# Eighteen of a layer's 96 gathered dot products split into a product on GpSimd and a sum on ScalarE, and the gate stage begun four blocks sooner

## The chip, the core and the metric

The program runs on one core of a Trainium2 chip. The metric is the device time of one execution in microseconds. In the profile the engines are PE (TensorE matmuls), PEld (its weight loads), DVE (VectorE), ACT (ScalarE), POOL (GpSimd) and SP (SyncE, which here only issues DMAs).

## What is computed

A trunk of two layers over 256 tokens of width 1024. Each layer has a mixer (attention and pooling in layer 0, a gated MLP in layer 1) and then a product-key channel mixer with 16384 experts, which takes most of the time and is the only part the change touches:

```python
q = (ht @ w_q).reshape(T, PEER_HEADS, 2, PEER_HALF_DIM)
scores = jnp.einsum('thic,hikc->thik', q, sub_keys)
sv, si = lax.top_k(scores, PEER_TOPK)
cand = sv[:, :, 0, :, None] + sv[:, :, 1, None, :]
best, ci = lax.top_k(cand.reshape(T, PEER_HEADS, 256), PEER_TOPK)
expert = (i1 * 128 + i2).reshape(T, 128)          # 8 heads x 16 picks
gate = jax.nn.softmax(best, axis=-1).reshape(T, 128)
hid = jax.nn.gelu(jnp.einsum('cd,ckd->ck', xb, w_down[eb]))
out = jnp.einsum('ck,ckd->cd', gb * hid, w_up[eb])
```

## The kernel before, in words

**Dense and gathered tokens.** Of the 256 tokens, 160 are handled densely: TensorE multiplies them with all 16384 experts, in 128 "down" blocks of 128 experts (`down(b)`, eight matmuls of 160 columns, which the trace counts as 16), and later 128 "up" blocks. The other 96 tokens are handled through gathered rows: 64 of them (two half-sets of picks on 128 partitions, 64 rows of the ring, "sparse") and 32 "later" tokens (four partitions sets, 32 rows, "more"). For each of these 96 rows GpSimd issues an indirect DMA that brings 128 expert rows of 1024 floats (512 KB) into a slot of a ring of ten (`gather(q)`), and VectorE takes one dot product per partition with `scalar_tensor_tensor` and an accumulator (`dots`, L1548). The other factor is `h_rows` in PSUM for sparse rows and `more_rows` in SBUF for more rows. In the up stage 96 more rows are gathered and added up with their coefficients (L1665).

**How a down block is handed on.** Three PSUM banks serve the down blocks in turn. `down(b)` waits until block b-3 has been taken out of its bank. In ScalarE's loop over b, the step for b first takes block b-2 through Gelu (`take_hidden(b - 2)`, L849, up to block `G_FROM - 1`; `activate_hidden`, L854, from there on), and then does what is hung on that b: the exponentials at b = 18 and 54 (`EXP_AT`), the row numbers, ten `write_ones` from b = 16 (`ONES_FROM` = 12 plus 4), the take-over of the later tokens' row numbers at b = 33, and so on. ScalarE also issues the odd loads of the down weights from n = 40 on.

**Retrieval on VectorE.** While TensorE goes through the down blocks, VectorE finds the picks, first of token tile 0 and then of tile 1. Tile 0's picks give the row numbers. During tile 1 there are 14 places at which some dots are put between the retrieval's instructions (`early_dot`): four in the first top-16 search, two in the second, eight in the loop that looks up the pick numbers (`L1601`). Place i does the dots up to `early_after(i)`. In total `EARLY` = 40 are done there, 18 sparse rows and then 22 of the later tokens' rows.

**The gate stage.** When both tiles are found (`idg_done`), TensorE turns numbers and gates round ahead of block `IDS_AT` = 77, VectorE splits them into two indices (`ids_split`), and from block `G_FROM` = 80 on, each down block is followed by the gates of four tokens (`token_gates(g)`, four matmuls of one-hot operands), 40 groups in all, to block 119. A group's operands are made by GpSimd (`build_first`, L629), ScalarE (`finish_one_hots`) and VectorE. The remaining 56 dots are spread over the blocks from `G_FROM` + 1 on, 56 in 44 blocks (`dots_after`).

**GpSimd's order.** In each layer it first asks for `EARLY + RING - 1` = 49 rows, then builds the operands of group 0, 1, ..., with later gathers between. `gather(q)` for q of 10 or more waits until row q-10, which had the slot, has been used, and until row q-5 has landed:

```python
for q in range(asked):
    gather(q)
pool.wait_ge(ids_split, l + 1)
for g in range(TGROUPS):
    build_first(g)
```

Lines printed by the profile: L613 gather, L629 first one-hots on GpSimd, L849 and L854 hidden values on ScalarE, L982 all matmuls, L596 the subtraction of two 128x1024 tiles on GpSimd in the mixer.

Of the kernel before, what the change touches and what calls it, by code (L numbers as in the profile page):

```python
# [16 lines left out]
LAYERS = 2  # L17
# [59 lines left out]
IDS_AT = 77  # L77
# [4 lines left out]
G_FROM = 80  # L82
# [3 lines left out]
ONES_FROM, ROWS_AT, ONES = 12, 8, 432  # L86
# [16 lines left out]


def row_of(n):

    if SPARSE_FIRST <= n < EARLY:
        return True, n - SPARSE_FIRST
    if n >= ROWS - MORE_LAST:
        return True, n - PICKS  # L110
    return False, n if n < EARLY else n - MORE + MORE_LAST
# [57 lines left out]
assert EXTRA_AT + EXTRA_SOON * DM <= QT_AT and EXTRA_AT + EXTRA * DM <= G_FROM * DENSE  # L169
# [20 lines left out]
def build_trunk(nc, x_d, gam_d, gfin_d, tab_d, ident_d, iota_d, lncount_d, poolm_d, poolw_d,  # L190
                pscale_d, wm_d, ws_d, bs_d, cnorm_d, subk_d, wd_d, wu_d, gff_d, sel_d, rows_d, up_rows_d, out_d):
    ctx = ExitStack()
    with ctx:
# [244 lines left out]
        def _(sp):  # L438
            for l in range(LAYERS):
# [147 lines left out]
        def _(pool):  # L587
            for l in range(LAYERS):
# [10 lines left out]
                def gather(q):  # L599
                    s, _, last = uses[q + l * GATHERS]  # L600
                    if last is not None:
                        pool.wait_ge(row_used, last + 1)
# [12 lines left out]
                    ).then_inc(row_full[s], 16)  # L615

# [37 lines left out]
        def _(act):  # L654
# [47 lines left out]
            for l in range(LAYERS):  # L702
# [182 lines left out]

                def finish_one_hots(g):
# [32 lines left out]
                for b in range(RAW, BLOCKS):  # L919
# [26 lines left out]
                act.wait_ge(row_used, l * GATHERS + ROWS)  # L946
# [24 lines left out]
            act.wait_ge(row_used, LAYERS * GATHERS)  # L971
# [8 lines left out]
        def _(pe):  # L980
# [54 lines left out]
            for l in range(LAYERS):  # L1035
# [287 lines left out]
                pe.wait_ge(row_used, (l + 1) * GATHERS)  # L1323
# [9 lines left out]
        def _(dve):  # L1333
# [64 lines left out]
            for l in range(LAYERS):  # L1398
# [155 lines left out]
                def early_dot(t):  # L1554
                    if t:
# [3 lines left out]
                        dots(early_after(early[0] - 1), early_after(early[0]))  # L1559
# [94 lines left out]
                def axpy(n):  # L1654
# [138 lines left out]
```

## Time and profile before

| what | us |
|---|---|
| median of 3 runs | 1523.56 |
| lowest and highest run | 1521.96, 1524.58 |
| the profiled execution, its own time | 1525.66 |
| its span, first to last instruction | 1523.9 |

The profiled execution lies 2.1 us above the median of the runs, and its span 1.8 us below its own time. Times in the rows are microseconds from the span's start. The second layer's blocks can be compared with the first's: `take_hidden(38)` and `take_hidden(75)` stand 737.24 us apart in the two layers.

### The profile page before, as it was taken

How to read it: one execution, taken by the hardware profiler on the slowest of the kernel's cores; microseconds unless marked ns; L12 is line 12 of the kernel's file. 1: busy time of each engine (PE TensorE's matmuls, PEld its weight loads, DVE VectorE, ACT ScalarE, POOL GpSimd, SP SyncE). 2: the span in 40 equal slices, each digit the busy share in tenths (PEclk: the TensorE clock that was granted, in tenths of full speed). 3: DMA queues.
4: the chain of work that ended last, by engine and by line, in shares of the span. 5: the costliest groups of instructions: out<-in, count | busy, mean ns of one | idle time of the engine just before them, and what ended most of it. 6: DMA issues, size and time to landing. Idle time of an engine off the chain costs nothing.

```text
span 1523.9 us, 29071 instructions
## 1 busy us (share of the span) xinstructions
PE 1488.1 (98%) x10668; PEld 1447.6 (95%) x10668; DVE 886.8 (58%) x2900; ACT 476.8 (31%) x1199; POOL 715.8 (47%) x632
## 2 busy tenths in 40 slices
PE   8999999999999999999999999999999999999997
PEld 6789989999999999999977999999999999999996
DVE  1740889947885444444623339997488934444472
ACT  5654231238881000000055533121688500000001
POOL 6567033347995223333467731333599723333340
PEclk9999999999999999999999999999999999999999
DMA  7456988999999999999854579999999999999992
GB/s 251 133 190 226 328 311 325 408 408 348 387 381 404 415 417 416 416 416 415 359 193 152 199 250 339 331 410 409 345 369 390 383 417 415 416 417 417 418 406 101
DMA packets 126560, 523.12 MB, mean 343 GB/s; under 512 B 14960, under 2 KB 15216, under 8 KB 109680
## 3 DMA queue, kind: packets, MB, share of 16 engines
q1 hardware_dynamic: 57328, 240.62, 41.5%
q0 software_dynamic: 55296, 201.35, 33.9%
q10 hardware_dynamic: 13824, 79.70, 12.8%
q8 instruction: 65, 1.06, 0.3%
q14 instruction: 47, 0.39, 0.1%
HBM read 519.48 MB, written 1.05 MB: 342 GB/s over the span
## 4 chain that ended last, share of the span: by engine, by line
PE 94%; ACT 2%; issue 1%; DVE 1%; DMA 1%; POOL 1%; SPq 0%; DVEq 0%; ACTq 0%; POOLq 0%
PE ps L982 93%; PE ps L990 1%; DMA raw<-in_wm 1%; ACT arena L671 1%; POOL w_lo L596 1%; ACT hT_hi L698 1%; DVE rtmp L1356 0%; ACT w_hi L683 0%; ACT arena L736 0%; DVE arena L1369 0%; ACT L661 0%; PE ps L1105 0%; DVE arena L1493 0%; PE ps L1304 0%; DVE hT_lo L1464 0%
## 5 line engine op out<-in xcount | busy, mean ns | idle before, releaser
L982 PE MATMUL ps<-arena,w_raw 128*128 128x160 f32 (+1 forms) x2688 | 380.1, 300 | 3.3 <-issue 3.2
L982 PE MATMUL ps<-arena,raw 128*128 128x160 f32 (+1 forms) x2688 | 379.1, 300 | 0.2
L982 PEld LDWEIGHTS ps<-arena,w_raw 128*128 128x128 f32 x2688 | 369.8, 191 | 4.5 <-issue 4.4
L982 PEld LDWEIGHTS ps<-arena,raw 128*128 128x128 f32 x2688 | 369.8, 191 | 0.7 <-issue 0.7
L613 POOL DMA_INDIRECT arena<-in_up_rows,ret x192 | 187.1, 974 | 358.6 <-DVE oh_buf L1665 264.3
L613 POOL DMA_INDIRECT arena<-in_rows,ret x192 | 199.9, 1041 | 296.0 <-ACT ret L871 104.5
L1665 DVE SCALAR_TENSOR_TENSOR oh_buf<-arena,ret,oh_buf 128x1024 f32<-128x1024 f32 x126 | 161.9, 1285 | 228.7 <-DMA arena<-in_up_rows,ret 213.8
L596 POOL TENSOR_TENSOR w_lo<-raw,w_hi 128x1024 fp32r<-128x1024 f32 x80 | 194.2, 2436 | 94.2 <-PE ps L982 66.1
L982 PE MATMUL ps<-arena 128*128 128x160 f32 (+5 forms) x1336 | 187.4, 304 | 2.7 <-issue 1.4
L982 PEld LDWEIGHTS ps<-arena 128*128 128x128 f32 (+2 forms) x1336 | 179.7, 190 | 7.3 <-issue 4.1
L1548 DVE SCALAR_TENSOR_TENSOR arena<-arena,ps 128x1024 f32<-128x1024 f32 x128 | 153.6, 1213 | 0.0
L961 ACT ACTIVATE arena<-ident 128x768 f32<-128x768 f32 x2 | 1.7, 842 | 448.4 <-PE ps L982 225.0
L629 POOL TENSOR_SCALAR oh_buf<-iota,ret 128x128 f32<-128x128 f32 x160 | 127.2, 802 | 13.3 <-PE ps L982 9.8
L849 ACT ACTIVATE arena<-ps 128x160 f32<-128x160 f32 x160 | 48.4, 303 | 269.9 <-PE ps L982 253.8
L1665 DVE SCALAR_TENSOR_TENSOR ret<-arena,ret 128x1024 f32<-128x1024 f32 x62 | 82.0, 1323 | 62.4 <-DMA arena<-in_up_rows,ret 54.4
L683 ACT ACTIVATE w_hi<-raw 128x1024 fp32r<-128x1024 f32 x80 | 83.8, 1062 | 73.8 <-DMA raw<-in_wm 46.4
L894 ACT ACTIVATE ret<-iota,ret 128x128 f32<-128x128 f32 x320 | 100.8, 386 | 4.1 <-PE ps L982 4.0
L1601 DVE SCALAR_TENSOR_TENSOR arena<-iota,ret,ps 128x54 f32<-128x54 f32 x512 | 100.5, 264 | 1.2 <-issue 1.2
L1548 DVE SCALAR_TENSOR_TENSOR arena<-arena,spare 128x1024 f32<-128x1024 f32 x64 | 76.7, 1217 | 19.2 <-DMA arena<-in_rows,ret 19.2
L982 PE MATMUL ps<-oh_buf,ret 128*128 128x128 f32 x640 | 84.8, 275 | 2.9 <-issue 2.8
L1646 DVE TENSOR_TENSOR arena<-arena,ps 128x512 f32<-128x512 f32 x80 | 54.9, 687 | 56.2 <-PE ps L982 50.7
L982 PEld LDWEIGHTS ps<-oh_buf,ret 128*128 128x128 f32 x640 | 79.5, 191 | 4.0 <-issue 4.0
(144 smaller groups left out, 1779.4 us busy)
## 6 DMA issues: line engine op xcount, KB each, us to landing
raw<-in_wd SPq DMA_DIRECT2D x92, 512.0 KB
w_raw<-in_wd SPq DMA_DIRECT2D x92, 512.0 KB
raw<-in_wm SPq DMA_DIRECT2D x80, 512.0 KB
low_rows<-in_wu SPq DMA_DIRECT2D x18, 1024.0 KB
arena<-in_wu SPq DMA_DIRECT2D x18, 1024.0 KB
arena<-in_wd SPq DMA_DIRECT2D x32, 512.0 KB, 5.0
raw<-in_wu SPq DMA_DIRECT2D x14, 1024.0 KB
raw<-in_wu ACTq DMA_DIRECT2D x14, 1024.0 KB
```

The costliest lines, as they stand in the source:

```text
L596: nc.gpsimd.tensor_tensor(w_lo[:, s % WLO, :], raw[:, s, :], whs[:, s].bitcast(F32), ALU.subtract).then_inc(wlo_pool, 1)
L613: nc.gpsimd.indirect_dma_start(ring[s], None, table, bass.IndirectOffsetOnAxis(ap=index, axis=0)).then_inc(row_full[s], 16)
L629: nc.gpsimd.tensor_scalar(oh1g[:, g % 2, k, :], iota[:, :], i1T[:, t:t + 1], gT[:, t:t + 1], ALU.is_equal, ALU.mult).then_inc(oh1_pool, 1)
L671: nc.scalar.activation(junk[:, t, ks], src[:, t, ks], ACT.Square, accum_out=sumsq[:, k, t:t + 1]).then_inc(sumsq_done, 1)
L683: nc.scalar.activation(whs[:, s], raw[:, s, :], ACT.Copy).then_inc(whi_done, 1)
L849: nc.scalar.activation(block_of(b), down_psum(b % SLOTS), ACT.Gelu_apprx_tanh).then_inc(h_done, 1)
L894: nc.scalar.activation(oh2[:, g % 2, k, :], iota[:, :], ACT.Abs, scale=-1.0, bias=i2T[:, t:t + 1]).then_inc(oh2_far, 1)
L982: return nc.tensor.matmul(out, lhsT, rhs, start=start, stop=stop, skip_group_check=shared)
L1548: nc.vector.scalar_tensor_tensor(row, row, 1.0, more_rows if more else h_rows, ALU.mult, ALU.mult, accum_out=(more_hid if more else row_hi ...
L1601: step(nc.vector.scalar_tensor_tensor(found[:, (j * 8 + k) % 24, :], places, cif[:, t, n:n + 1], pay[:, h, :], ALU.is_equal, ALU.mult, acc ...
L1646: nc.vector.tensor_tensor(part, part, gates, ALU.mult).then_inc(gmul_done, 1)
L1665: ins = nc.vector.scalar_tensor_tensor(out, row, coef[:, j:j + 1], out, ALU.mult, ALU.add)
```

## The change

`BY_POOL` = 18 of the 32 later tokens' rows are no longer dotted by VectorE. GpSimd multiplies the row in its ring slot with `more_rows` (in place), and ScalarE sums the product with an `ACT.Copy` with accumulator. GpSimd does the product of row q-5 just after `gather(q)` (`POOL_AFTER` = 5). ScalarE does sum j at b = `SUM_AT[j]`, which is 40, 42, 44, 46, 48, 49, 51, 53, 54, 56, 58, 59, 61, 63, 65, 66, 68, 70, after `take_hidden(b - 2)`. A ring slot of such a row is free after its sum.

The order of rows becomes: 18 sparse rows (positions 0 to 17), then the rows for GpSimd at positions 18, 20, 22, 24 and 26 to 39 with four sparse rows between (19, 21, 23, 25), then the other 42 sparse rows and the last 14 of the later tokens'. `EARLY` stays 40, but only 22 of these are VectorE's, so the 14 places hold 1, 2, 1, 2, 1, 2, 2, 1, 2, 1, 2, 1, 2, 2 dots instead of two or three each. `IDS_AT` goes from 77 to 73, `G_FROM` from 80 to 76; the remaining 56 dots take 48 blocks. `write_ones` moves from b = 16 on to b = 34 on, and has one piece more. The places that waited for all dots wait for VectorE's and, where it matters, for the sums.

```diff
-IDS_AT = 77
+IDS_AT = 73
-G_FROM = 80
+G_FROM = 76
-ONES_FROM, ROWS_AT, ONES = 12, 8, 432
+ONES_FROM, ROWS_AT, ONES = 30, 8, 432
-SPARSE_FIRST, MORE_LAST = 18, 10
-EARLY, EARLY_PLACES = SPARSE_FIRST + MORE - MORE_LAST, 14
+SPARSE_FIRST, BY_POOL, BETWEEN, POOL_AFTER = 18, 18, 4, 5
+EARLY, EARLY_PLACES = SPARSE_FIRST + BY_POOL + BETWEEN, 14
+DVE_ROWS = GATHERS - BY_POOL
+def row_order():
+    order = [(False, j) for j in range(SPARSE_FIRST)]
+    for j in range(BY_POOL):
+        order.append((True, j))
+        if j < BETWEEN:
+            order.append((False, SPARSE_FIRST + j))
+    order += [(False, j) for j in range(SPARSE_FIRST + BETWEEN, PICKS)]
+    return order + [(True, j) for j in range(BY_POOL, MORE)]
+ROW_ORDER = row_order()
+POOL_ROWS = [n for n in range(EARLY) if ROW_ORDER[n][0]]
+EARLY_DOTS = [n for n in range(EARLY) if not ROW_ORDER[n][0]]
+SUM_AT = [40 + 23 * j // 10 if j < BETWEEN else 48 + 17 * (j - BETWEEN) // 10 for j in range(BY_POOL)]
 def dots_after(b):
-    return EARLY + max(0, min(ROWS - EARLY, (b - G_FROM - 1) * (ROWS - EARLY) // 44))
+    return EARLY + max(0, min(ROWS - EARLY, (b - G_FROM - 1) * (ROWS - EARLY) // 48))
 def early_after(i):
-    return (i + 1) * EARLY // EARLY_PLACES
+    return (i + 1) * len(EARLY_DOTS) // EARLY_PLACES
...
+        def row_free(n):
+            l, q = n // GATHERS, n % GATHERS
+            if q in POOL_ROWS:
+                return more_summed, l * BY_POOL + POOL_ROWS.index(q) + 1
+            return row_used, l * DVE_ROWS + dots_before(q) + 1
...
                 def gather(q):
                     s, _, last = uses[q + l * GATHERS]
                     if last is not None:
-                        pool.wait_ge(row_used, last + 1)
+                        pool.wait_ge(*row_free(last))
...
+                def more_products(q):
+                    slot, filled, _ = uses[q + l * GATHERS]
+                    pool.wait_ge(more_rows_sb, 16 * PARTS * (l + 1))
+                    pool.wait_ge(row_full[slot], 16 * (filled + 1))
+                    nc.gpsimd.tensor_tensor(ring[slot], ring[slot], more_rows, ALU.mult).then_inc(more_product, 1)
...
                 for q in range(asked):
                     gather(q)
+                    if q - POOL_AFTER in POOL_ROWS:
+                        more_products(q - POOL_AFTER)
...
+                def sum_products(j):
+                    slot = uses[POOL_ROWS[j] + l * GATHERS][0]
+                    act.wait_ge(more_product, l * BY_POOL + j + 1)
+                    nc.scalar.activation(ring[slot], ring[slot], ACT.Copy,
+                                         accum_out=more_hid[:, j:j + 1]).then_inc(more_summed, 1)
...
                     if b == MORE_TAKE_AT:
                         take_more_picks()
+                    if b in SUM_AT:
+                        sum_products(SUM_AT.index(b))
```

## Rows read from the trace of the kernel before

**Rows 1.** The page: busy us of each engine, its share, instructions.
```profile
PE 1488.1 (98%) x10668; PEld 1447.6 (95%) x10668; DVE 886.8 (58%) x2900; ACT 476.8 (31%) x1199; POOL 715.8 (47%) x632
```
**Rows 2.** The page: the chain of work that ended last, by engine.
```profile
PE 94%; ACT 2%; issue 1%; DVE 1%; DMA 1%; POOL 1%; SPq 0%; DVEq 0%; ACTq 0%; POOLq 0%
```
**Rows 3.** TensorE's waits, the largest: us in total, times, longest.
```profile
PE ps L982 <- issue: 7.4, 13, 2.2
```
**Rows 4.** TensorE in order of time, layer 1's first gate group: start, length.
```profile
1083.04 1.19 PE L982 MATMUL ps<-oh_buf,ret 128*128 128x128 f32 x8 [2.24 <-issue]
1084.02 4.00 PE L982 MATMUL ps<-arena,raw 128*128 128x160 f32 x16
1087.86 1.05 PE L982 MATMUL ps<-oh_buf,ret 128*128 128x128 f32 x8
```
**Rows 5.** GpSimd in order of time, the last early gather, layer 1.
```profile
1080.36 0.94 POOL L613 DMA_INDIRECT arena<-in_rows,ret  x1 [1.61 <-DMA arena<-in_rows,ret]
1081.35 4.70 POOL L629 TENSOR_SCALAR oh_buf<-iota,ret 128x128 f32<-128x128 f32 x6
```
**Rows 6.** Windows: length, busy (count) PE, PEld, DVE, ACT, POOL, clock, DMA share, GB/s.
```profile
1080.80:1083.00 2.20, 0.00 (x0) 0.00 (x0) 0.00 (x0) 0.90 (x3) 2.15 (x4) 1.00 1.04 415
1084.00:1085.00 1.00, 1.00 (x6) 1.00 (x5) 0.64 (x2) 0.73 (x3) 1.00 (x2) 0.50 1.01 401
```
**Rows 7.** ScalarE's time order: hidden 38, layer 0; hidden 38, 41, 75, layer 1.
```profile
251.55 0.30 ACT L849 ACTIVATE arena<-ps 128x160 f32<-128x160 f32 x1 [1.87 <-issue]
...
988.79 0.30 ACT L849 ACTIVATE arena<-ps 128x160 f32<-128x160 f32 x1 [1.87 <-PE ps L982]
...
995.31 0.30 ACT L849 ACTIVATE arena<-ps 128x160 f32<-128x160 f32 x1 [1.34 <-PE ps L982]
...
1069.20 0.30 ACT L849 ACTIVATE arena<-ps 128x160 f32<-128x160 f32 x1 [1.87 <-PE ps L982]
```
**Rows 8.** VectorE's time order: place 1, layer 0; places 1, 7, 9, layer 1.
```profile
224.76 1.21 DVE L1548 SCALAR_TENSOR_TENSOR arena<-arena,ps 128x1024 f32<-128x1024 f32 x1
...
964.44 1.22 DVE L1548 SCALAR_TENSOR_TENSOR arena<-arena,ps 128x1024 f32<-128x1024 f32 x1
965.58 0.09 DVE L1548 DVE_READ_ACCUMULATOR arena<-arena,ps 128x1 f32 x1
...
1011.02 1.21 DVE L1548 SCALAR_TENSOR_TENSOR arena<-arena,ps 128x1024 f32<-128x1024 f32 x1
...
1022.88 1.21 DVE L1548 SCALAR_TENSOR_TENSOR arena<-arena,spare 128x1024 f32<-128x1024 f32 x1
```
**Rows 9.** GpSimd's time order: the mixer's subtraction, layer 0; two gathers, layer 1.
```profile
51.66 2.42 POOL L596 TENSOR_TENSOR w_lo<-raw,w_hi 128x1024 fp32r<-128x1024 f32 x1 [2.62 <-PE ps L982]
...
982.13 0.94 POOL L613 DMA_INDIRECT arena<-in_rows,ret  x1 [6.73 <-DVE arena L1548]
983.37 0.94 POOL L613 DMA_INDIRECT arena<-in_rows,ret  x1 [0.30 <-DVE arena L1548]
```
**Rows 10.** The page, groups: busy, mean ns of one, idle before and its releaser.
```profile
L596 POOL TENSOR_TENSOR w_lo<-raw,w_hi 128x1024 fp32r<-128x1024 f32 x80 | 194.2, 2436 | 94.2 <-PE ps L982 66.1
L683 ACT ACTIVATE w_hi<-raw 128x1024 fp32r<-128x1024 f32 x80 | 83.8, 1062 | 73.8 <-DMA raw<-in_wm 46.4
```
**Rows 11.** ScalarE in order of time, b = 54 of layer 1 (exponential).
```profile
1017.41 1.28 ACT L924 ACT_TABLE_LOAD   x1
...
1019.04 1.28 ACT L849 ACT_TABLE_LOAD   x1
```
**Rows 12.** GpSimd and VectorE at the same time, end of layer 0.
```profile
745.45 5.65 POOL L596 TENSOR_TENSOR w_lo<-raw,w_hi 128x1024 fp32r<-128x1024 f32 x2 [2.27 <-PE ps L982]
...
746.64 2.24 DVE L1665 SCALAR_TENSOR_TENSOR ret<-arena,ret 128x1024 f32<-128x1024 f32 x1 [2.46 <-DMA arena<-in_up_rows,ret]
```
**Rows 13.** VectorE in order of time beside GpSimd's subtraction, layer 0.
```profile
51.60 0.68 DVE L1434 SCALAR_TENSOR_TENSOR arena<-ps,arena 128x512 f32<-128x512 f32 x1
```
**Rows 14.** Windows, columns as in rows 6: the gate stage, layer 1.
```profile
1110.00:1130.00 20.00, 20.00 (x159) 20.00 (x158) 17.65 (x36) 16.82 (x53) 18.15 (x21) 1.00 0.99 381
```

More of the change, by code:

```diff
@@ L85, with dots_before @@
 G_TO = G_FROM + TGROUPS
-ONES_FROM, ROWS_AT, ONES = 12, 8, 432
-SPARSE_FIRST, MORE_LAST = 18, 10
-EARLY, EARLY_PLACES = SPARSE_FIRST + MORE - MORE_LAST, 14
+ONES_FROM, ROWS_AT, ONES = 30, 8, 432
[14 more added lines that the diff above has]
+SUM_AT = [40 + 23 * j // 10 if j < BETWEEN else 48 + 17 * (j - BETWEEN) // 10 for j in range(BY_POOL)]
+def dots_before(q):
+    return q - sum(n < q for n in POOL_ROWS)
 def dots_after(b):
-    return EARLY + max(0, min(ROWS - EARLY, (b - G_FROM - 1) * (ROWS - EARLY) // 44))
+    return EARLY + max(0, min(ROWS - EARLY, (b - G_FROM - 1) * (ROWS - EARLY) // 48))
 def early_after(i):
-    return (i + 1) * EARLY // EARLY_PLACES
+    return (i + 1) * len(EARLY_DOTS) // EARLY_PLACES
 def row_of(n):
[L107 to L111, printed above, removed]
+    return ROW_ORDER[n]
 def up_row_of(n):
@@ L168 @@
 EXTRA_AT, EXTRA_SOON = 4608, 4
-assert EXTRA_AT + EXTRA_SOON * DM <= QT_AT and EXTRA_AT + EXTRA * DM <= G_FROM * DENSE
+assert EXTRA_AT + EXTRA_SOON * DM <= QT_AT and ONES_FROM + RAW - 2 >= WIDE_TO - 1
 assert all(WIDE + DOWN_RAW + k <= (EXTRA_AT + k * DM) // DENSE for k in range(EXTRA))
@@ L382, in build_trunk @@
         row_used = sem("row_used")
+        more_product, more_summed = sem("more_product"), sem("more_summed")
         hid_done = sem("hid_done")
@@ L548, in load_first @@
                     load_up(p, p)
-                sp.wait_ge(row_used, l * GATHERS + ROWS - ROWS % RING)
+                sp.wait_ge(row_used, l * DVE_ROWS + dots_before(ROWS - ROWS % RING))
                 load_up(RING_PAIR, RING_PAIR)
                 load_first(RAW_PAIRS)
-                sp.wait_ge(row_used, l * GATHERS + ROWS)
+                sp.wait_ge(row_used, l * DVE_ROWS + dots_before(ROWS))
+                sp.wait_ge(more_summed, (l + 1) * BY_POOL)
                 load_up(SPARE_PAIR, SPARE_PAIR)
@@ L945, in _ @@
                     load_between(b)
-                act.wait_ge(row_used, l * GATHERS + ROWS)
+                act.wait_ge(more_summed, (l + 1) * BY_POOL)
+                act.wait_ge(row_used, l * DVE_ROWS + dots_before(ROWS))
                 nc.scalar.activation(both_hid, both_hid, ACT.Gelu_apprx_tanh).then_inc(hid_done, 1)
@@ L970, in _ @@
                                          ACT.Copy).then_inc(upT_done, 1)
[L971 removed]
+            act.wait_ge(row_used, LAYERS * DVE_ROWS)
             norm_stats(xs, vn, x_ready, 8 * LAYERS - 4, order=((1, 0), (0, 0), (1, 1), (0, 1)))
@@ L1322, in _ @@
                         turn_back(g - 1)
-                pe.wait_ge(row_used, (l + 1) * GATHERS)
+                pe.wait_ge(row_used, (l + 1) * DVE_ROWS)
                 for k in range(2):
@@ L1540, in wait_row, with dots @@
                     dve.wait_ge(row_full[slot], 16 * (filled + 1))
-                def dots(first, last):
-                    for q in range(first, last):
+                def dots(first, last, rows=range(ROWS)):
+                    for q in rows[first:last]:
                         wait_row(q)
@@ L1558, in early_dot @@
                             dve.wait_ge(more_rows_sb, 16 * PARTS * (l + 1))
-                        dots(early_after(early[0] - 1), early_after(early[0]))
+                        dots(early_after(early[0] - 1), early_after(early[0]), EARLY_DOTS)
                         early[0] += 1
```

2 lines of the change are left out of this document (1 added, 1 removed).

## The prediction

> **What bounds the kernel now.** I read the busy line first: TensorE is busy for 1488.1 of 1523.9 us, VectorE for 58% and GpSimd for 47% [rows 1]. Then the chain that ended last: 94% of it is TensorE [rows 2]. So relief of VectorE is worth only what TensorE waits for VectorE, and any new wait of TensorE costs its full length. TensorE's own waits are small: 7.4 us in 13 waits, the longest 2.2 us [rows 3]. That longest one is at the change's place: in layer 1 the first gate group starts after 2.24 us of idling, and the block behind it takes 3.84 us (1084.02 to the next group at 1087.86) [rows 4]. The reader is to see in the windows that the clock was at 0.50 (1.2 GHz) after this gap and at 1.00 (2.4 GHz) ahead of it [rows 6]. What was late is GpSimd: its last early gather began at 1080.36, waiting for an earlier row to land, and only then came the one-hots [rows 5]. The pace of a down block is otherwise 2.173 us: hidden 38 at 988.79 and hidden 75 at 1069.20, 80.41 us for 37 blocks [rows 7]. So the incident costs 2.24 + (3.84 - 2.17) and 0.14 for the slow group (1.19 against 1.05), 4.1 us; layer 0 has none.
>
> **The change part by part.** *ScalarE's new wait* decides. At b = 40 ScalarE takes hidden 38 and then waits for GpSimd's first product. Behind that wait in its order stands hidden 39, and `down(42)` needs hidden 39 out of its bank. So TensorE can finish block 41 (995.31 less a launch, say 995.3 [rows 7]) and no more until product 0 is summed. When is product 0 made? It is of position 18, and GpSimd does it after `gather(23)`. `gather(23)` needs the slot of row 13, so VectorE's 14th dot. With 1, 2, 1, 2, 1, 2, 2, 1, 2 dots in the first nine places, the 14th is the last dot of place 9, the third place in the look-up loop. Before, place 9 began at 1022.88 with 22 dots ahead of it [rows 8]; now 12 are ahead. A dot is 1.14 us (964.44 to 965.58 [rows 8]), so place 9 begins 10 x 1.14 = 11.4 us sooner, at 1011.5, and its two dots end at 1013.8. (None of the first nine places waits for data in between: their rows were asked for 10 rows ahead.) `gather(22)` has gone at 1012.9, `gather(23)` ends at 1015.1, at 0.94 + 0.30 us each [rows 9]. The product is GpSimd's `tensor_tensor` on 128x1024 floats: the trace has no in-place one, its nearest row is the subtraction of the same size, 2436 ns mean and 2.42 us alone [rows 9, 10]; I take 2.4. Product 0 is there at 1017.8. The sum is a 128x1024 `ACTIVATE`, 1.06 us [rows 10]; hidden 39 follows and TensorE goes on at 1019.3. **First wait: 1019.3 - 995.3 = 24.0 us in layer 1.** In layer 0 place 1 is at 224.76 (739.68 earlier) and hidden 38 at 251.55 (737.24 earlier) [rows 7, 8], so the same wait is 2.4 us shorter: 21.6 us.
>
> *The next sums.* Product 1 needs `gather(25)`, row 15, place 11; product 2 row 17, place 12; product 3 row 19, place 13. The look-up between two places takes 3.08 us without dots (1011.02 to 1022.88 is 11.86 us for two gaps and 5 dots of 1.14 [rows 8]). With 1.5 dots a place that makes products at 1026.1, 1031.5 and 1036.7. From there GpSimd alone sets the pace: a gather and a product, 0.94 + 0.30 + 2.40 + 0.30 = 3.94 us, so product 4 at 1041.8 and product 7 at 1053.7. Each sum frees ScalarE 1.1 us later, and TensorE, at most three blocks ahead, waits again: 4.0 us ahead of block 44, then 1.0, 0.8, 0.8 and 1.8 us to block 51. At b = 54 the exponential with two table loads takes 2.9 us [rows 11] and now comes on top of a late sum: 2.1 us more. Behind that a sum is due every 1.7 blocks, 3.7 us, against 3.94: 0.4 us more. Sum: 10.9 us a layer. The restarts: a block at half clock costs 1.7 us extra [rows 4, 6]. Up to block 51 GpSimd is the later of the two and hides it; I count one in each layer less a little, 1.5 us. Bounds: none, and two full ones (3.4).
>
> *The dots off VectorE.* 18 x 1.14 = 20.5 us fewer, in retrieval. Retrieval then ends at about 1038.3 instead of 1070.5, far ahead of block 73, which TensorE now reaches near 1100. This hides VectorE's part wholly; its worth is nothing, since the one wait it could remove is the gate stage's.
>
> *Numbers and gates four blocks sooner.* No instruction is added for TensorE. GpSimd ends product 17 at 1093 and its 49th gather at about 1098; TensorE is at block 76 at 1107. So the 4.1 us of layer 1 go [rows 4]. In the gate stage there are 56 dots in 48 blocks in place of 44, and four more hidden products; VectorE was busy 17.65 of 20 us there and TensorE 20.00 [rows 14]: 0. In the last 12 blocks, now without gates, a block of 524 KB in 2.17 us (241 GB/s) and 1.17 gathers of the same size (282) want more than the 415 GB/s seen when the DMAs are full [rows 6], covered by up to nine rows asked ahead: 0 to 2 us a layer, I take 0. `write_ones` has the form of the old one and falls in or beside ScalarE's long wait: 0.
>
> *The sum.* Layer 1: 24.0 + 10.9 + 1.5 - 4.1 = 32.3. Layer 0: 21.6 + 10.9 + 1.5 = 34.0. Together 66.3 us. On the profiled execution, 1525.66 + 66.3 = 1592; it lay 2.1 above the median of the runs, so **1590 us**.
>
> *Do the two engines hinder each other?* At the end of layer 0 GpSimd's subtractions took 5.65 us for two, 2.83 each, while a VectorE operation with both inputs in SBUF took 2.24 us instead of 1.28 [rows 12]. But with one input in PSUM, VectorE's L1434 kept 0.68 us beside a subtraction of 2.42 [rows 9, 13]. The look-ups and the sparse dots have one input in PSUM, so I take 2.4 and no slowing. The Trainium skill (Perfetto Trace Analysis, Optimizing Scalar/DVE Operations) warns that the two share an SBUF read port, so that moving operations between them "might not help". By that warning taken at its full width the sum would be the rival's below; the page SBUF — State Buffer (Summary: rules for kernel authors) narrows it to operations with two SBUF inputs, and by that the sum above stands.
>
> **The rivals.**
> - *Hindrance.* Products at 2.83 us and VectorE's look-ups and dots 1.3 times as long while products run. Period 4.37 instead of 3.94, over 17 products 7 us, and the dots that free the slots for products 1 to 3 about 4 us later: 11 to 12 us a layer more, 1590 + 23 = 1613. For it: rows 12. Against it: rows 13.
> - *Only the gate stage is late.* If product 0 were ready near b = 40, the 49 gathers would still wait for rows to land, the DMAs full [rows 5, 6], and end as before, while TensorE wants group 0 four blocks, 8.7 us, sooner. Layer 1: 2.2 + 8.7; layer 0: up to 8.7. With two slow restarts (3.4) and less the old 4.1: +19 at most, 1543. Against it: the 14th dot's place.
> - *Faster.* One mechanism: product 0 is made by 989, so ScalarE never holds TensorE, and the gathers run ahead; then the 4.1 us of layer 1 are gained, 1519.5. It decides at place 9: it would have to begin some 28 us sooner than computed. Nothing in the rows gives that.
> - *The later chain is quicker* (products 2.2 us, gaps 0.16): 7.5 us less over both layers, 1582; with the first waits alone, +41.5, 1565.
>
> **How the numbers follow.** Forecast (both long waits and GpSimd's pace behind) 0.78, hindrance 0.12, only gate stage 0.06, faster 0.02, no change 0.02. Time of the likeliest: 1590. Its own spread is from 1565 (first waits alone) to 1597 (two restarts, 2 us tail in each layer). The range 1565 to 1614 takes hindrance in and leaves the gate-stage and faster cases out. Within 0.2% (3 us) is what a measurement here can hardly tell from nothing. Faster 0.02, same 0.02, slower 0.96.
>
> **What the profile after would show.** ScalarE's longest wait on GpSimd 26 to 29 us once in each layer, just after hidden 38, at about 252 and 989 + 34; TensorE idle 22 to 24 us there, its clock at 0.50 for some us behind it, then four to six waits of 1 to 4 us; 36 products of 2.4 us and as many sums of 1.06; no wait ahead of the first gate group; the up stage unchanged. I am wrong if the wait after hidden 38 is short, if products take 3 us, or if TensorE still waits at group 0.

## The result, and the profile after

The kernel after takes 1577.88 us (median of 4 runs, 1576.14 to 1579.43), the kernel before beside it 1524.07 (4 runs, 1521.96 to 1528.28): ratio 1.0361, 95% interval 1.0334 to 1.0388, 3.6% slower. The forecast was 1590 in a range of 1565 to 1614. The profiled execution of after took 1579.22 us, with a span of 1577.4, 53.5 us above the span of before.

The forecast is 12 us too high, inside its range. The page of the kernel after, the lines that answer to [rows 1] and [rows 2], and the group of the products:

```profile
PE 1490.8 (95%) x10668; PEld 1448.7 (92%) x10668; DVE 849.2 (54%) x2836; ACT 514.9 (33%) x1273; POOL 794.2 (50%) x668
...
PE 79%; issue 8%; POOL 5%; ACT 3%; DMA 3%; DVE 1%; SPq 0%; POOLq 0%; DVEq 0%; ACTq 0%
...
L650 POOL TENSOR_TENSOR arena<-arena,spare 128x1024 f32<-128x1024 f32 x36 | 85.2, 2367 | 0.6
```

VectorE lost 37.6 us of work, and TensorE has the same 10668 instructions. What changed is TensorE's share of the chain: 79% in place of 94%, with GpSimd in it at 5%. The waits of the kernel after (engine, line, who for: total, times, longest), where the largest group of TensorE's matmuls in before was 7.4 us [rows 3]:

```profile
ACT arena L926 <- POOL arena L650: 114.3, 30, 27.2
...
PE ps L1028 <- ACT arena L886: 49.2, 6, 23.0
PE ps L1028 <- issue: 6.5, 16, 1.4
```

ScalarE waits for products (L650) at its sums (L926), 30 times of 36, and TensorE waits for ScalarE's hidden rows (L886). The place is seen in three time orders of layer 1. ScalarE:

```profile
1017.72 0.30 ACT L886 ACTIVATE arena<-ps 128x160 f32<-128x160 f32 x1 [1.22 <-PE ps L1028]
1017.92 0.55 ACT L899 ACTIVATE arena<-ident 128x432 f32<-128x432 f32 x1
1045.69 1.06 ACT L926 ACTIVATE arena<-arena 128x1024 f32<-128x1024 f32 x1 [27.21 <-POOL arena L650]
1046.74 0.28 ACT L886 ACTIVATE arena<-ps 128x160 f32<-128x160 f32 x1
```

GpSimd: gathers 22 and 23 and product 0, and then two steps of the steady chain:

```profile
1041.10 0.94 POOL L642 DMA_INDIRECT arena<-in_rows,ret  x1 [3.27 <-DVE arena L1594]
1042.34 0.94 POOL L642 DMA_INDIRECT arena<-in_rows,ret  x1 [0.30 <-DVE arena L1594]
1043.29 2.37 POOL L650 TENSOR_TENSOR arena<-arena,spare 128x1024 f32<-128x1024 f32 x1
...
1083.13 0.98 POOL L642 DMA_INDIRECT arena<-in_rows,ret  x1 [0.16 <-issue]
1084.14 2.36 POOL L650 TENSOR_TENSOR arena<-arena,spare 128x1024 f32<-128x1024 f32 x1
1086.66 0.98 POOL L642 DMA_INDIRECT arena<-in_rows,ret  x1 [0.16 <-issue]
1087.66 2.37 POOL L650 TENSOR_TENSOR arena<-arena,spare 128x1024 f32<-128x1024 f32 x1
```

TensorE, at that wait, and at the first gate group (against [rows 4]):

```profile
1047.17 6.88 PE L1028 MATMUL ps<-arena,raw 128*128 128x160 f32 x32 [22.97 <-ACT arena L886]
1055.50 4.58 PE L1028 MATMUL ps<-arena,w_raw 128*128 128x160 f32 x32 [1.45 <-issue]
...
1130.16 2.34 PE L1028 MATMUL ps<-arena,w_raw 128*128 128x160 f32 x16
1132.34 1.05 PE L1028 MATMUL ps<-oh_buf,ret 128*128 128x128 f32 x8
1133.23 2.34 PE L1028 MATMUL ps<-arena,w_raw 128*128 128x160 f32 x16
```

Windows of after in layer 1, columns as in [rows 6]: behind the long wait, and in the gate stage (against [rows 14]):

```profile
1048.00:1050.00 2.00, 2.00 (x10) 2.00 (x9) 2.00 (x15) 0.12 (x1) 0.00 (x0) 0.50 0.80 254
...
1160.00:1180.00 20.00, 20.00 (x159) 20.00 (x158) 16.71 (x37) 16.43 (x51) 18.10 (x21) 1.00 0.99 350
```

The reader is to see: hidden 38 is taken, ScalarE stands for 27.21 us before product 0, TensorE for 22.97, and the two blocks behind it take 6.88 us in place of 4.35, with the clock at 0.50 up to about 1052 (0.54 in the window 1050 to 1052, 1.00 in 1052 to 1054). In layer 0 the same wait is 21.64 us. The first gate group has no wait any more.

**Where the 53.5 us are.** A clean measure is the way from ScalarE's `take_hidden(38)` to the first gate group. In e9 below, which has no wait there, it is 82.82 us in layer 1 (82.83 in layer 0) with `G_FROM` = 76, and in e8, also without a wait, 91.52 us with 80 (four blocks of 2.173 more). Above that, after loses 31.8 us in layer 1 (114.62 us from 1017.72 to 1132.34) and 30.5 in layer 0; before loses 2.7 in layer 1 (94.25 us) and nothing in layer 0. The rest: the gate stage, first group to last, takes 119.60 us in both layers of after, against 120.45 (layer 0) and 122.21 (layer 1) in before, so -0.85 and -2.61. Everything else, from layer 0's start to the up stage of layer 1, differs by -2.5. Sum: 30.5 + 31.8 - 2.7 - 0.85 - 2.61 - 2.5 = 53.6.

### The profile page after: what moved, and what is told of

It reads as the page before. It is cut to its first block, busy times and chain, and to the rows that moved or that the text cites. A ratio compares the mean times of both kernels' runs of the same rounds, so it can differ in the third digit from the quotient of the medians.

```text
span 1577.4 us, 29165 instructions
## 1 busy us (share of the span) xinstructions
PE 1490.8 (95%) x10668; PEld 1448.7 (92%) x10668; DVE 849.2 (54%) x2836; ACT 514.9 (33%) x1273; POOL 794.2 (50%) x668
## 4 chain that ended last, share of the span: by engine, by line
PE 79%; issue 8%; POOL 5%; ACT 3%; DMA 3%; DVE 1%; SPq 0%; POOLq 0%; DVEq 0%; ACTq 0%
PE ps L1028 78%; POOL arena L642 3%; POOL arena L650 2%; DMA arena<-in_rows,ret 2%; PE ps L1036 1%; DMA raw<-in_wm 1%; DMA spare<-in_wu 1%; ACT arena L708 1%; POOL w_lo L625 1%; ACT hT_hi L735 1%; ACT L886 0%; ACT L967 0%; DVE rtmp L1402 0%; ACT w_hi L720 0%; ACT arena L773 0%
## 5 line engine op out<-in xcount | busy, mean ns | idle before, releaser
L1028 PE MATMUL ps<-arena,raw 128*128 128x160 f32 (+1 forms) x2688 | 384.1, 302 | 47.6 <-ACT arena L886 46.8
L642 POOL DMA_INDIRECT arena<-in_rows,ret x192 | 193.1, 1006 | 241.5 <-ACT ret L908 102.7
L886 ACT ACTIVATE arena<-ps 128x160 f32<-128x160 f32 x152 | 44.2, 299 | 163.6 <-PE ps L1028 138.0
L650 POOL TENSOR_TENSOR arena<-arena,spare 128x1024 f32<-128x1024 f32 x36 | 85.2, 2367 | 0.6
L1028 PE MATMUL ps<-arena,spare 128*128 (+1 forms) x576 | 82.2, 299 | 0.0
```

Source lines behind the costliest of these rows:

```text
L642: nc.gpsimd.indirect_dma_start(ring[s], None, table, bass.IndirectOffsetOnAxis(ap=index, axis=0)).then_inc(row_full[s], 16)
L650: nc.gpsimd.tensor_tensor(ring[slot], ring[slot], more_rows, ALU.mult).then_inc(more_product, 1)
L886: nc.scalar.activation(block_of(b), down_psum(b % SLOTS), ACT.Gelu_apprx_tanh).then_inc(h_done, 1)
L1028: return nc.tensor.matmul(out, lhsT, rhs, start=start, stop=stop, skip_group_check=shared)
```

## The experiments

Twelve kernels in four sets, each set on one chip. The kernel before, run beside them, took 1523.36 us in the set of e1 to e4, 1521.25 in that of e5 to e7, 1513.38 in that of e8 to e10 and 1522.69 in that of e11 and e12. So ratios and traces are compared across sets, not times, and the times that were expected are to be read beside a before of about 1523 us. The loss in the table is that on the way to the gates in layer 1, as just defined. e11, the kernel before once more, is told at e8.

| kernel | us (median) | ratio to before, 95% interval | loss on the way to the gates, layer 1 |
|---|---|---|---|
| after | 1577.88 | 1.0361 (1.0334 to 1.0388) | 31.8 |
| e1: dots sooner | 1555.31 | 1.0217 (1.0199 to 1.0234) | 19.8 |
| e2: no product | 1569.06 | 1.0310 (1.0293 to 1.0327) | 25.2 |
| e3: gates back | 1586.85 | 1.0430 (1.0407 to 1.0453) | 32.8 |
| e4: before, gates sooner alone | 1534.78 | 1.0094 (1.0066 to 1.0122) | 8.1 |
| e5: e3, late rows from PSUM | 1583.33 | 1.0381 (1.0334 to 1.0429) | 32.8 |
| e6: dots sooner, sums later | 1536.46 | 1.0085 (1.0054 to 1.0117) | 9.8 |
| e7: product one gather behind | 1601.26 | 1.0511 (1.0466 to 1.0557) | 39.3 |
| e8: before, one-hots first | 1512.62 | 0.9993 (0.9984 to 1.0002) | 0.0 |
| e9: all retimed | 1510.89 | 0.9985 (0.9976 to 0.9994) | 0.0 |
| e10: sums later alone | 1552.89 | 1.0268 (1.0252 to 1.0283) | 18.5 |
| e12: e8 again | 1519.40 | 0.9981 (0.9959 to 1.0003) | 6.4 |

**e1, the early dots sooner.** The kernel after with

```diff
 def early_after(i):
-    return (i + 1) * len(EARLY_DOTS) // EARLY_PLACES
+    return min(len(EARLY_DOTS), (i + 1) * EARLY // EARLY_PLACES)
```

> The changed kernel with VectorE's 22 early dots put as early as before (2, 3, 3, 3, 3, 3, 3, 2 in the first eight places, none in the last six) instead of 1 or 2 in each. Theory (ScalarE waits for product 0, which waits for the 14th dot): the 14th dot moves from the ninth place to the fifth, so in layer 1 from 1043 - 1.1 to about 1030, TensorE's wait ahead of block 42 falls from 23.0 to about 10.3 us, product 7 comes 15 us sooner, and both layers together give back about 31 us: 1547 us (1542 to 1553). Rival (GpSimd's products are too slow, or the two engines hinder each other): the chain behind the first wait is what counts, and the time stays within 8 us of 1578.

Measured 1555.31, 22.6 us less: far outside the rival's 8 us, so the place of the 14th dot counts, but 2 us above the theory's range, and 22.6 saved where about 31 were expected. The first wait of layer 1 is 11.59 us, not 10.3, that of layer 0 12.2, and behind them 8.2 us a layer are lost, nearly the 8.8 of after. VectorE in order of time beside GpSimd's product 1 shows one cause of what is lost behind:

```profile
1026.13 2.77 DVE L1635 CAST ret<-ret 128x128 f32<-128x128 uint32 x1
```

```profile
1026.44 2.37 POOL L650 TENSOR_TENSOR arena<-arena,spare 128x1024 f32<-128x1024 f32 x1
```

The same cast took 0.22 us in layer 1 of before and in e7, where no product ran beside it. Here it ends at 1028.90, just behind the product's end at 1028.81. It makes the next dot late, and with it product 2. Layer 0 of e9 shows the same in another size; VectorE, and GpSimd beside it:

```profile
271.03 0.91 DVE L1639 CAST ret<-ret 128x128 f32<-128x128 uint32 x1
```

```profile
269.47 2.38 POOL L650 TENSOR_TENSOR arena<-arena,spare 128x1024 f32<-128x1024 f32 x1
```

The cast came in the middle of the product and ended at 271.94, again just behind the product's end at 271.85. The Trainium skill (SBUF — State Buffer, Who interferes with whom) counts casts and copies among the VectorE operations that can lock a port pair shared with GpSimd, so that the one that comes second waits for the other's end. e9 agrees with that. In e1 the cast also ends with the product, but by the recorded starts it was the first of the two, by 0.31 us, with a gather on GpSimd up to 1026.42; what held it in these 0.31 us is not shown.

**e2, sums and waits kept, the products' time taken away.**

```diff
-nc.gpsimd.tensor_tensor(ring[slot], ring[slot], more_rows, ALU.mult).then_inc(more_product, 1)
+nc.gpsimd.tensor_tensor(ring[slot][:, 0:8], ring[slot][:, 0:8], more_rows[:, 0:8], ALU.mult).then_inc(more_product, 1)
```

> The changed kernel with GpSimd's products cut to the first 8 of 1024 columns (the rest of the product is left out, so the sums of these rows are wrong). All waits stay. Theory (the 14th dot is late): the first wait only loses the 2.2 us of the product, 23.0 to 20.8 in layer 1 and 21.6 to 19.4 in layer 0, and the GpSimd-paced waits behind it lose 3 to 4 us: 6 us a layer, 1566 us (1561 to 1571). Rival (product time or hindrance is the cause): nearly all of the 54 us is given back, under 1540 us.

Measured 1569.06. With nearly all of the products' 85.2 us gone, 8.8 us are gained; the first wait of layer 1 is still 20.01 us. That is inside the theory's range. So it is not the size of the product that costs, but when it may begin.

**e3, the numbers and gates back at 77 and 80,** the dots again over 44 blocks.

```diff
-IDS_AT = 73
+IDS_AT = 77
-G_FROM = 76
+G_FROM = 80
-(b - G_FROM - 1) * (ROWS - EARLY) // 48
+(b - G_FROM - 1) * (ROWS - EARLY) // 44
```

> The changed kernel with the numbers and the gates back at blocks 77 and 80 (56 dots in 44 blocks). Theory: TensorE comes late to these blocks anyway and finds everything ready, so the four blocks are worth nothing either way: 1578 us (1575 to 1581). Rival (the earlier gate stage costs or gains something of its own, through 12 gateless blocks at the end in which loads and gathers want more than the DMAs give): a difference of 4 us or more.

Measured 1586.85, 9.0 us more, the rival's side. The theory that the four blocks are worth nothing falls. The gate stage takes 122.75 and 122.73 us in place of 119.60, and the trace shows it at its end. TensorE and GpSimd in e3, layer 0:

```profile
485.34 1.13 PE L1028 MATMUL ps<-oh_buf,ret 128*128 128x128 f32 x8 [1.25 <-issue]
...
489.11 1.13 PE L1028 MATMUL ps<-oh_buf,ret 128*128 128x128 f32 x8 [0.46 <-issue]
```

```profile
478.62 1.59 POOL L664 TENSOR_SCALAR oh_buf<-iota,ret 128x128 f32<-128x128 f32 x2
...
486.48 2.53 POOL L664 TENSOR_SCALAR oh_buf<-iota,ret 128x128 f32<-128x128 f32 x2
```

GpSimd's two one-hots of a group take 2.53 us instead of 1.59, from the point where VectorE's dots come to the later tokens' rows, which have both inputs in SBUF. In after the gates end four blocks sooner, and most of these rows come behind them.

**e5, e3 with these rows' second input in PSUM.**

```diff
-row, row, 1.0, more_rows if more else h_rows, ALU.mult, ALU.mult,
+row, row, 1.0, h_rows, ALU.mult, ALU.mult,
```

> The kernel after with the gates' four blocks put back (the same kernel as the run with IDS_AT 77, G_FROM 80 and dots over 44 blocks, which took 1586.9 us), and in it the 14 late dots of more_rows read h_rows (in PSUM) instead of more_rows (in SBUF), so these 14 values are those of other rows; the number and the size of the instructions are the same. Theory (in that run GpSimd's one-hots grow from 1.59 to 2.53 us beside dots with two operands in SBUF, in the last four gate groups, and the gate stage from 119.60 to 122.75 us): without such dots the gate stage is 119.6 us again, and the time 2 x 3.15 less, 1580.5 us (1578 to 1583). Rival (the stage is longer because 5 more dots per layer have to go into fewer blocks, or because TensorE's blocks end in another order): the gate stage stays at 122 to 123 us and the time at 1585 to 1589.

Measured 1583.33, between the theory's range and the rival's, with before at 1521.25 beside it. The ratios of e3 and e5 overlap too much to decide; the trace decides. GpSimd in e5 at the same place:

```profile
485.94 1.59 POOL L664 TENSOR_SCALAR oh_buf<-iota,ret 128x128 f32<-128x128 f32 x2
...
488.77 1.59 POOL L664 TENSOR_SCALAR oh_buf<-iota,ret 128x128 f32<-128x128 f32 x2
```

The one-hots are back at 1.59 us, no wait over 0.6 us is left at the last groups, and the gate stage is 120.46 us in both layers. So 2.3 of the 3.15 us per layer were the two engines hindering each other. The other 0.86 goes with the gates' place: the stage takes 119.6 us where the gates begin at block 76 and nothing holds it (after, e2, e4), and 120.2 to 120.5 where they begin at block 80 (before in layer 0, e5, e8, e11). Why is open. e5 still has 32.8 us of loss ahead of the gates in layer 1, as e3: about 1 us of those belongs to the later gates, the rest to the sums.

**e4, the other part alone: before with the numbers and gates four blocks sooner.**

```diff
-IDS_AT = 77
+IDS_AT = 73
-G_FROM = 80
+G_FROM = 76
-ONES_FROM, ROWS_AT, ONES = 12, 8, 432
+ONES_FROM, ROWS_AT, ONES = 30, 8, 432
-(b - G_FROM - 1) * (ROWS - EARLY) // 44
+(b - G_FROM - 1) * (ROWS - EARLY) // 48
```

> The kernel before with only the second part of the change: numbers at block 73, gates from block 76, the ones written later, 56 dots in 48 blocks; all dots stay on VectorE. Theory: GpSimd ends its 49 gathers as late as before (341.2 and 1082.9 us with group 0's one-hots) while TensorE wants them 8.7 us sooner; layer 0 waits about 7 us and layer 1 11, with a slow restart in each: 17 us more than before, 1541 us (1535 to 1545). Rival (TensorE's stage can be moved for nothing, since GpSimd's gathers speed up while TensorE waits): within 5 us of before.

Measured 1534.78, just under the theory's range, but by another wait than the theory's: not for GpSimd at group 0. TensorE waits 5.92 and 6.33 us ahead of turning the numbers round, for VectorE, whose retrieval still holds all 40 early dots and in layer 1 waits 2.25 us for a row just before its end, and 1.6 us in each layer in the twelve last blocks. So the relief of VectorE and the sooner gates go together: the sooner gates alone cost 11.4 us in before, and to take them out of after costs 9.0 (e3).

**e7, the same wait from the other side: products sooner in GpSimd's order.**

```diff
-SPARSE_FIRST, BY_POOL, BETWEEN, POOL_AFTER = 18, 18, 4, 5
+SPARSE_FIRST, BY_POOL, BETWEEN, POOL_AFTER = 18, 18, 4, 1
```

> The kernel after with POOL_AFTER 1 instead of 5: product 0 (row 18) stands behind gather 19 on GpSimd, not behind gather 23, and so on; dots, sums and their blocks unchanged. Theory (the first wait is gather 23's wait for the 14th dot): product 0 starts at 1032.5 instead of 1043.3 in layer 1 (gather 19 at 1031.5 waits for the 10th dot, two places earlier), the first wait is 10.8 us shorter in each layer, and the time 1556 us (1551 to 1561). Rival (the product waits for its row's landing, or GpSimd's period of 3.5 us sets the chain whatever the order, so that what the first wait gives back the later ones take): 1565 to 1580, with ScalarE's later waits over 2 us.

Measured 1601.26: the rival's side, and beyond its range. The first waits did shorten as the theory had it, to 12.30 and 10.76 us. But now each product waits for its own row. GpSimd in e7, layer 1:

```profile
1044.89 0.98 POOL L642 DMA_INDIRECT arena<-in_rows,ret  x1 [0.16 <-issue]
1046.77 0.94 POOL L642 DMA_INDIRECT arena<-in_rows,ret  x1 [0.91 <-DVE arena L1594]
1050.77 2.36 POOL L650 TENSOR_TENSOR arena<-arena,spare 128x1024 f32<-128x1024 f32 x1 [3.06 <-DMA arena<-in_rows,ret]
```

Row 20 is asked for at 1044.89 and is there at 1050.77, 5.9 us later. GpSimd, in order, asks for no further row meanwhile, so every later product pays the landing too, and seven waits of 1.0 to 3.9 us follow in layer 1. A distance of one gather is too short; distances between one and five were not tried.

**e10, only the sums moved.** The kernel after with

```diff
-SUM_AT = [40 + 23 * j // 10 if j < BETWEEN else 48 + 17 * (j - BETWEEN) // 10 for j in range(BY_POOL)]
+SUM_AT = [53, 57, 59, 62] + [60 + j for j in range(BETWEEN, BY_POOL)]
```

> The kernel after with the sums alone moved to later blocks (53, 57, 59, 62, 64, 65 ... 77), dots as in after. Theory (two things cost: ScalarE's order ahead of the products, and behind it GpSimd's own chain, which VectorE's 14th dot starts and 3.52 us a product continue, ending at 1111.2 us in layer 1 of after): the first wait goes, but TensorE meets the chain's end at the gates instead: group 0 at 1111.2 + 3.75 + 1.6 = 1116.6 where after has 1132.3 (15.7 us saved), 12.3 us in layer 0 by the same sum; the time is 1550 us (1545 to 1556). Rival 1 (ScalarE's order is all): the time falls by all of the waits, under 1540. Rival 2 (the chain sets all, the order nothing): 1568 to 1578.

Measured 1552.89. That lies in the expected range, but before takes 1513.38 on this chip, 10.7 us less than beside after; the ratio of 1.0268 would be 1564 beside a before of 1523. By the traces 13.3 us of loss are gone in layer 1 and 12.0 in layer 0 (30.5 to 18.5), where 15.7 and 12.3 were expected, and 2.2 to 2.3 us a layer come back in the gate stage (121.92 and 121.79 us for 119.60), whose first group and block run at half clock behind the wait. The span is 26.4 us shorter than that of after, of which some 5.6 lie in places that the edit doesn't touch. The ratio fell by 0.0093, or 14 us; what after would take on this chip was not measured. TensorE's waits in e10 at the end of the way, layer 1:

```profile
1089.85 3.97 PE L1028 MATMUL ps<-arena,raw 128*128 128x160 f32 x16 [4.35 <-ACT arena L886]
...
1105.74 2.05 PE L1028 MATMUL ps<-oh_buf,ret 128*128 128x128 f32 x8 [9.74 <-POOL oh_buf L664]
```

The wait behind hidden 38 is gone, and a wait for GpSimd's one-hots stands at the first gate group. (The 4.35 us ahead of it are for ScalarE, where a late sum and a fill of 3776 columns, 3.33 us, stand ahead of a hidden block.) So the theory of two costs, one hidden behind the other, holds: ScalarE's order costs 12 to 13 us a layer on the way, and behind it GpSimd's chain, begun late by VectorE's 14th dot, holds the other 18.5.

**e6, both: dots as in e1, and sums later.**

```diff
-SUM_AT = [40 + 23 * j // 10 if j < BETWEEN else 48 + 17 * (j - BETWEEN) // 10 for j in range(BY_POOL)]
+SUM_AT = [44, 46, 50, 52] + [54 + 17 * (j - BETWEEN) // 10 for j in range(BETWEEN, BY_POOL)]
```

> The kernel after with the early dots taken at the kernel before's pace (22 dots by place 7 instead of 13) and with every sum at a later block, where its product is ready (44, 46, 50, 52, 54, 55, 57 ... 76 instead of 40, 42, 44, 46, 48, 49, 51 ... 70). Theory (the whole loss is that ScalarE stands in its own order ahead of hidden rows which TensorE needs, for products that come later): neither of the 12 us waits is left, nor the later ones of 0.8 to 1.5 us except that at the exponentials, and the time falls by 44.6 (first waits of after), 6 (later waits) and 3 (blocks at half clock), to 1524 us (1519 to 1532), within 0.5% of the kernel before. Rival 1 (the products hold up VectorE in the look-up, as its cast of 2.77 us beside a product shows, or GpSimd ends its gathers after block 76): a wait of 5 to 15 us per layer comes back at the first gate group, 1535 to 1555. Rival 2 (products and sums cost by their load): over 1555.

Measured 1536.46, a little above the theory's range and inside rival 1's, though with a wait of 3.3 us at group 0 and not 5 to 15. TensorE's two largest groups of waits in e6:

```profile
PE ps L1028 <- ACT arena L886: 7.1, 2, 3.8
PE ps L1028 <- ACT ret L945: 6.6, 2, 3.3
```

The first group is sum 0, placed too soon (ScalarE waits 8.21 us at it in layer 1). The second is at group 0. The profile puts it down to ScalarE, and the theory of e9 below takes it so, but ScalarE's part of group 0 was done at 1086.23. TensorE and GpSimd in e6, layer 1:

```profile
1089.38 2.05 PE L1028 MATMUL ps<-oh_buf,ret 128*128 128x128 f32 x8 [3.33 <-ACT ret L945]
```

```profile
1086.70 0.94 POOL L642 DMA_INDIRECT arena<-in_rows,ret  x1 [0.30 <-issue]
1087.69 3.14 POOL L664 TENSOR_SCALAR oh_buf<-iota,ret 128x128 f32<-128x128 f32 x4
```

The first two of these four one-hots, group 0's, end at about 1089.3, and TensorE begins 0.1 us behind them; in layer 0 and in e10 the distance is the same. So the end of GpSimd's chain is what group 0 waits for here too. Of the 44.6 us of first waits 37.5 are gone.

**e9, retimed by what these traces show.** The kernel after with four dots a place, the sums where GpSimd's 3.52 us allow them, the numbers at block 70, and two groups' one-hots ahead of GpSimd's last gathers:

```diff
-    return (i + 1) * len(EARLY_DOTS) // EARLY_PLACES
+    return min(len(EARLY_DOTS), (i + 1) * 4)
...
-SUM_AT = [40 + 23 * j // 10 if j < BETWEEN else 48 + 17 * (j - BETWEEN) // 10 for j in range(BY_POOL)]
+SUM_AT = [47, 49, 52, 54] + [56 + 16 * (j - BETWEEN) // 10 for j in range(BETWEEN, BY_POOL)]
...
-IDS_AT = 73
+IDS_AT = 70
...
+                    if q == asked - 5:
+                        pool.wait_ge(ids_split, l + 1)
+                        build_first(0)
+                        build_first(1)
-                pool.wait_ge(ids_split, l + 1)
                 for g in range(TGROUPS):
-                    build_first(g)
+                    if g > 1:
+                        build_first(g)
```

> The kernel after, retimed so that no engine stands ahead of another's work: early dots 4 a place (22 by place 6), the sums at the blocks where their products are ready by GpSimd's 3.52 us (47, 49, 52, 54, 56, 57, 59 ... 76), the picks' numbers at block 70, and the one-hots of groups 0 and 1 ahead of GpSimd's last four early gathers. Theory (in the run with front dots and late sums, 13.8 us were left in four waits of 3.3 to 3.8 us, two at sum 0, which came some four blocks too soon, and two at group 0, where ScalarE's long fill and last sum stood ahead of its one-hots): these waits go, and the time is that of the kernel before less its 4.1 us and up to 4 us more where a sum is still off by a block: 1522 us (1518 to 1529). Rival (VectorE's late start of the look-up, or products at the place of the split, bring back 3 to 8 us a layer): 1530 to 1540.

Measured 1510.89 against 1513.38 of before on the same chip: ratio 0.9985 (0.9976 to 0.9994). The expected 1518 to 1529 was reckoned beside a before of 1523, where this ratio would give 1521. TensorE has no wait between hidden 38 and the last gate group, in either layer. TensorE in e9, layer 1:

```profile
1064.80 2.34 PE L1032 MATMUL ps<-arena,w_raw 128*128 128x160 f32 x16
1066.97 1.05 PE L1032 MATMUL ps<-oh_buf,ret 128*128 128x128 f32 x8
1067.86 2.34 PE L1032 MATMUL ps<-arena,w_raw 128*128 128x160 f32 x16
```

All 36 products and sums are still in it. So the whole loss of the kernel after was their order and timing. e9 has four edits at once; which of them the last few microseconds need was not tried one by one. It is 2.5 us faster than before beside it; its gate stage takes 119.60 and 119.71 us where e8 has 120.45 and 120.44.

**e8, e11, e12: is there something to gain in before?** e8 is before with

```diff
 for q in range(asked):
     gather(q)
+    if q == asked - 3:
+        pool.wait_ge(ids_split, l + 1)
+        build_first(0)
+        build_first(1)
-pool.wait_ge(ids_split, l + 1)
 for g in range(TGROUPS):
-    build_first(g)
+    if g > 1:
+        build_first(g)
```

> The kernel before with one edit: GpSimd builds the one-hots of groups 0 and 1 ahead of its last two early gathers instead of behind them. Theory (the 4.1 us of layer 1 are TensorE's wait for group 0's one-hots, which stand behind gathers that wait for rows to land): group 0 finds its one-hots ready, TensorE has no wait ahead of it in layer 1 and no block at half clock, and the time falls by 4.1 us, to 1519 us (ratio 0.997; 0.9955 to 0.999). Rival 1 (ScalarE's own one-hots of group 0 or VectorE's split end just as late): 0 to 1 us saved, ratio over 0.999. Rival 2 (the two gathers that now come 3 us later make VectorE's dots late): slower than before.

Measured 0.9993 (0.9984 to 1.0002): rival 1's result. e11 is before unchanged, for a second trace; e12 is e8 again, beside it.

> The kernel before unchanged, for a second trace of it: the fastest trace so far of a kernel built from it (one-hots of groups 0 and 1 first) lay 15 us under the first trace of before, while the times on that chip were level. Theory (the 2.24 us wait ahead of layer 1's first gate group, and TensorE's short idles of 0.3 to 1.0 us beside the first gathers of each layer, differ from execution to execution or chip to chip): this trace shows one or both in another size. Rival (they belong to the kernel): 2.2 us ahead of the group and the short idles at the same places again.

> The kernel before with GpSimd's one-hots of groups 0 and 1 ahead of its last two early gathers, a second time, beside a trace of before from the same chip. Theory: it saves what that trace shows of wait ahead of layer 1's first gate group and the block at half clock behind it, 4.1 us (0.27%) if the wait is 2.2 us again, nothing if the wait is absent. Rival: the ratio stays within 0.1% of 1 although the wait is there, since the later gathers give it back.

e11 took 1524.22 us in its one run. Its first gate group of layer 1:

```profile
1083.52 1.13 PE L982 MATMUL ps<-oh_buf,ret 128*128 128x128 f32 x8 [1.18 <-ACT ret L902]
1084.48 2.34 PE L982 MATMUL ps<-arena,raw 128*128 128x160 f32 x16
```

The wait is 1.18 us here, not 2.24, and no block at half clock follows. So the size of the 4.1 us of [rows 4] belonged to that execution, and a kernel without the wait can gain 1 to 4 us. e12 gives 0.9981 (0.9959 to 1.0003). Its own trace has another wait in layer 1, of 3.23 us for the end of VectorE's retrieval, ahead of turning the numbers round; the last early dot there waited 2.27 us for its row to land. Whether the edit is worth anything stays open.

## Why the prediction was right

Against the terms of its sum, from the traces of before and after (us):

| step | predicted, layer 0 and 1 | measured |
|---|---|---|
| first wait of TensorE | 21.6, 24.0 | 21.64, 22.97 |
| later waits and restarts | 12.4, 12.4 | 8.8, 8.8 |
| the old wait at layer 1's gates | -4.1 | -4.5 |
| gates four blocks sooner | 0, 0 | -0.85, -0.85 |
| all other places | 0 | -2.5 |
| sum | 66.3 | 53.5 |

- **ScalarE's new wait decides: shown.** Product 0 began behind gather 23, which waited for VectorE's 14th dot; the wait is there at the forecast place and length. e1 (the dots sooner), e7 (the product sooner) and e10 (the sum later) each shorten it by itself, from three sides.
- **The later waits and restarts: the terms that were mis-sized, 3.6 us a layer too high.** Three parts of it can be read from the trace.
  - GpSimd's pace. "A gather and a product, 0.94 + 0.30 + 2.40 + 0.30 = 3.94 us." It is 3.52: the product follows its gather at once (a gather's start to the product's, 1086.66 to 1087.66, is 1.00 us), and only 0.16 us lie behind it. The gap of 0.30 between two gathers was carried over to a pair that doesn't have it. Product 5 ended 26.8 us behind product 0, where the forecast has 27.9, and TensorE was released for block 51 with 7.2 us lost since its first wait, in both layers, where the sum has 8.4. That is 1.2 us.
  - The restart, 1.5 us, was counted twice. The two blocks behind the first wait took 2.5 us too long in layer 1, and the wait for sum 1 behind them was 1.45: together the 4.0 us that the sum has "ahead of block 44". Product 1 came when forecast, 8.3 us behind product 0, and TensorE at full clock would have waited for it too.
  - Behind block 51 1.6 us were lost, where the sum has 2.5 (exponential and tail): 0.9 us, which the quicker pace and the exponential share.
  The rival "the later chain is quicker" named 7.5 us and the right gap (0.16), but products of 2.2 us, which took 2.37. Its size is that of the whole miss of 7.2 us, by luck in part, since 3.0 of these are the restarts.
- **Hindrance: the rival fell for what it named, and is true in a place that the prediction left out.** Products took 2.37 us, and the dots with an input in PSUM kept 1.21 us. But "operations with two SBUF inputs" was too narrow a reading: e1's cast of 2.77 us has one. The row of the Trainium skill that the prediction cites (SBUF — State Buffer, Summary: rules for kernel authors) names VectorE's 2-port mode beside the two SBUF inputs. And one-hots beside dots with both inputs in SBUF took 2.53 us for 1.59 (e3, and e5 without them), where the prediction put the gate stage at 0.
- **The dots off VectorE, put at nothing: right here, and only while the order is wrong.** In e4 the gates sooner without this relief cost 11 us; in e9, with it and all waits gone, they cost none. That retrieval would end 49.5 us after hidden 38 (1038.3) missed a wait: in after it ended 65.4 us after it, at 1083.14, since VectorE stood 15.84 us for ScalarE's exponential, which was late too. TensorE wanted it at 1123.2 only, so this cost nothing.
- **The gates four blocks sooner, put at 0: half right.** TensorE had no wait there, but e3 shows 3.15 us a layer that the kernel after would pay without it. Against before it is 0.85 us a layer.
- **Only the gate stage is late (1543):** its place is right as a second bound, hidden behind the first: 9.7 us at group 0 in e10, 3.3 in e6. Its mechanism is not: what was late there was GpSimd's chain of products, which VectorE's 14th dot starts, and not gathers that wait for rows to land.
- **Faster (1519.5):** its condition, products ready when ScalarE comes, is what e9 makes, from the other end: the sums wait for the products' blocks. It gives 0.9985, about half of the 0.27% that the old wait promised; that wait differs between executions (e11).

## What to carry to other kernels

An engine that takes work in a fixed order passes every wait on to what stands behind it. Before hanging a new step into such a queue, work out when its input is ready, through every engine that it passes (here VectorE's dot, GpSimd's gather and product), and put it behind that time; otherwise moving work off a busy engine can cost more than it gives, as it did here. When the first wait is gone, look for the next one: here GpSimd's chain stood hidden behind ScalarE's order. And check the engine that a trace names for a wait against the times: in e6 it named ScalarE, which had been done for 3 us.

## What the runs showed of the hardware that was not expected

- A cast of 128x128 on VectorE took 2.77 us instead of 0.22 beside a product of GpSimd, to the product's end (e1, both layers), and 0.91 us in layer 0 of e9. Beside a gather alone it took 0.22 in layer 1 of e9.
- TensorE's clock: behind a wait of 2.24 us the next block ran at half clock (4.00 us, [rows 4, 6]); behind 1.18 us in e11, and behind 1.45 us in after, blocks ran at full clock (2.34 us, and two in 4.58). The length of the wait alone doesn't decide it. TensorE in e7, layer 1, two waits of nearly one length:

```profile
1061.88 6.26 PE L1028 MATMUL ps<-arena,w_raw 128*128 128x160 f32 x32 [2.65 <-ACT arena L886]
1070.66 4.58 PE L1028 MATMUL ps<-arena,raw 128*128 128x160 f32 x32 [2.52 <-ACT arena L886]
```

Behind the 2.65 us the granted clock was 0.55 (1062 to 1064), behind the 2.52 it was 1.00 (1070.7 to 1075), though the wait of 2.24 us in before brought 0.50.
- A row gathered by GpSimd was there for its product 5.9 us after it was asked for (e7), with the DMA engines busy for 75% of that time.
- Short idles of TensorE of 0.3 to 1.0 us between single matmuls, put down to "issue", stand near 210 us in the traces of before and e12 (3.2 and 2.5 us in all), as gaps of 0.2 to 0.4 in that of after, and not at all in those of e8 and e9. They are part of the -2.5 us above, and differ with the chip or the execution. Their cause was not tried.
